# Two gated feed-forward layers: the second pair of result tiles in the second group computed by seven products, the preparation in fewer steps

## The chip, the cores and the metric

The kernel runs on one core of a Trainium2 chip. The metric is the device time of one execution in microseconds. The core's engines are TensorE (PE in the profile, its weight loads PEld), VectorE (DVE), ScalarE (ACT), GpSimd (POOL) and SyncE (SP), each with an instruction queue of its own that runs in order; they wait for each other through semaphores.

## The reference

Two blocks on 512 tokens of width 1024, in float32, the second with two layers:

```python
def first_block(x, ...):        # attention, HGRN2 recurrence and MLA branches, gated and merged, then
    x = x + jnp.square(jax.nn.relu(rmsnorm(x) @ w_ff1)) @ w_ff2
def second_block(x, ...):       # 2 layers: stick-breaking attention, differential attention
    x = x + mix
    x = x + (silu(h @ w_gate[i]) * (h @ w_up[i])) @ w_down[i]      # h = rms_norm(x, ffn_norm[i])
```

`w_gate` and `w_up` are 1024 x 2816, that is 22 result tiles of 128 columns each. The change concerns the two gated layers, the order of work in the preparation of all three feed-forward layers, and one detail of the recurrence.

## The kernel before

Everything is computed transposed: a tile is 128 features x 512 tokens. Each float32 operand is split into a high part (float32r) and a low part (the rest), and a product is high x high, low x high and high x low: three matmuls for one.

**Plain tiles.** A result tile ("rows" unit) takes 8 tiles of 128 inputs, 24 matmuls of 512 columns, issued in four pieces of six. Its weights come as a chunk of 512 KB (`raw`); ScalarE makes the high part (`split`, L1723, tile `wh`), VectorE the low part (`split_low`, `wl`). A gate tile is scaled by VectorE (L2262), goes through ScalarE's three steps of the sigmoid and is multiplied (`ev3`, L2328); an up tile is scaled and multiplied by the gate (L2318); then the result is split (tiles `R`). Output tiles ("out" units) are added to x by VectorE (L2430).

**Sevens.** A pair of neighbouring result tiles can be computed as a 2 x 2 block product with seven products instead of eight (class `Seven`): each product is 12 matmuls of 256 columns, 84 for the pair instead of 96 of that size. It needs four sums of the weights (S1 to S4, GpSimd, L2761, in the buffers `Q`, two of them in turn, filled by a 1 MB transfer each) and four sums of the tokens (T1 to T4, `sums`), each with a high and a low part. The products are, in this order: A12·B21, A11·B11, A22·T4, S1·T1, S2·T2, S4·B22, S3·T3. The weights' high parts (`wo_hi`) are ScalarE's, their low parts (`wo_lo`, tiles `wx` and `hl`) VectorE's, in four places in turn, made two to three products ahead. Partial results are combined by both (`wcp`, `wc`), and `wsig`, `wf`, `wf_hi`, `wf_lo` make the function's value. Product 6 of a seven is issued one piece later than the others, behind the next piece or behind product 0 of the next seven.

**The order.** A planner writes one list of steps; each engine's program takes its own steps from it in that order. `dense` walks through the pieces of a stage; behind each piece it lists the low parts pending (`low`), the steps deferred until now (`due`), the extra steps of this piece's number, and the eviction. `hgrn` gives the steps of the recurrence, which run between the pieces of the first gate/up group (`uGA`).

**The feed-forward layers** are stage 0 (first block), 1 and 2. `chain` orders them: all plain tiles of groups 0 and 1, the outputs of group 0, then sevens and outputs in turn. In stages 1 and 2 group 0 has two result tiles each of gate and up, group 1 four, all plain: 12 plain units of four pieces, 48 pieces; then 8 output pieces; then the first product. In stage 0 there are 8 plain units (32 pieces), and 16 output pieces. `preparation` places, by piece number: eight normed token tiles (`hn`, L2351, into `Q1`), the token sums (`t_sum`, L2362), their high (`t_hi`) and low parts (`t_lo`), the high and low parts of B21, B11 and B22 (`b_hi`, `b_lo`, into `hh` and `hl`, free after the last plain tile), and the first weights. The transfer for the second seven (`wq`) needs `Q1` and so waits for all of `b_lo`. In stages 1 and 2 the low part of T4 is placed at step 58, at the third product.

Of the kernel before, what the change touches and what calls it, by code (L numbers as in the profile page):

```python
# [192 lines left out]

PRODUCTS = (("A12", "B21"), ("A11", "B11"), ("A22", "T4"), ("S1", "T1"), ("S2", "T2"), ("S4", "B22"), ("S3", "T3"))
WEIGHT_PART = {n: i for i, n in enumerate(("A11", "A12", "A22", "A21", "S1", "S2", "S4", "S3"))}
TOKEN_SUMS = ("T1", "T2", "T3", "T4")
TOKEN_PARTS = {"B21": (4, 0), "B11": (0, 0), "B22": (4, 1)}
TOKEN_ORDER = ("B21", "B11", "B22")

# [111 lines left out]
class Plan:  # L311
# [89 lines left out]
            self.defer(9 + tt, "dt", u, tt)  # L401
        self.defer(5, "dn_root", u)

    def dense(self, units, more=None, crossed=False, hold=0):

        n, order, held = 0, [], []
        for u in units:  # L410
            if u.kind == "win":
                pieces = [(k, 0, 0) for k in range(7)]
            elif u.kind == "rows":
                pieces = [(0, j * u.nk + k, j * u.nk + k + 2) for j in range(u.n) for k in range(0, u.nk, 2)]
            else:
                pieces = [(i, a, a + 2) for i in range(4) for a in range(0, 8, 2)]
            order += [(u, piece) for piece in pieces]
        if crossed:
            order = order[:3] + order[4:6] + order[3:4] + order[6:]
        for i in range(len(order) - 1, 0, -1):  # L420
            if order[i - 1][0].kind == "win" and order[i - 1][1][0] == 6:
                order[i - 1], order[i] = order[i], order[i - 1]
        for i, (u, piece) in enumerate(order):
            tick, extra = self.low() + self.due(), (more or {}).get(n, [])
            after = order[i + 1][0] if i + 1 < len(order) else u
            n += 1
            if u.kind == "win":
                yield [("wp", u, piece[0])], self.seven(u, piece[0]) + tick + extra
                continue
            self.place(u)  # L430
            if u.kind == "rows" and piece[2] % u.nk == 0:
                steps = self.ready(u, piece[2] // u.nk - 1)
                if u.ev == "out" and after.kind == "win" and after.stage and steps[0][0] == "split":
                    self.defer(2, *steps.pop(0))
                    self.defer(4, *self.lows.pop())
                if n <= hold:
                    held.append(steps.pop())
                    tick += steps + extra
                else:
                    self.gated(u)  # L440
                    tick += steps[:-1] + extra + steps[-1:]
            else:
                tick += extra
            if held and n > hold:
                tick.append(held.pop(0))
                self.gated(tick[-1][1])
            if u.halved(piece[1] // u.nk) and piece[2] % u.nk:
                tick += [("ev_half", u), ("ship_half", u)]
            if u.kind == "cols" and piece[2] == 8:
                if piece[0] == 3:  # L450
                    tick.append(("ev", u))
                    if u.ev == "dq":
                        self.heads(u)
                tick += self.split(u.chunks[piece[0]] + 2)
            yield [("mm", u, *piece)], tick
        rest = self.due(True)
        if rest:
            yield [], rest
# [32 lines left out]
    def preparation(self, v, stage, wins, tick):  # L491

        more, w = {}, wins[0].v
        last_up = self.last_up[stage]

        def put(n, *step):
            more.setdefault(n, []).append(step)

        put(tick + 3, "wq", wins[0])
        plain = stage == 0  # L500
        end = 32 if plain else 48
        for m in range(8):
            put(((13, 14, 16, 17, 18, 20, 21, 22) if plain else (14, 15, 17, 18, 20, 21, 23, 24))[m], "hn", v, stage, m)
        put(14, "ws", wins[0])
        for k in range(4):
            put(((22, 24, 25, 27) if plain else (26, 28, 30, 32))[k], "t_sum", stage, k)
            put(((24, 25, 27, 28) if plain else (28, 29, 31, 33))[k], "t_hi", stage, k)
            put(((28, 30, 38, 40) if plain else (34, 36, 39, 58))[k], "t_lo", stage, k)
        put(29, "wo_hi", 7 * w)
        put(31, "wo_lo", 7 * w)  # L510
        put(30, "wo_hi", 7 * w + 1)
        put(end + 10 if plain else end - 1, "wo_lo", 7 * w + 1)
        for i in range(3):
            put(end + i, "b_hi", stage, i, last_up)
            put(end + 2 + i, "b_lo", stage, i)
        put(end + (9 if plain else 10), "wq", wins[1])
        put(end + (9 if plain else 10), "ws", wins[1])
        put(end + 3, "wo_hi", 7 * w + 2)
        return more
# [111 lines left out]
    def make(self):  # L631
# [23 lines left out]
        for idx, ff, e, norm in ((0, ff2a, 4, 4), (1, ff2b, 6, None)):  # L655
            for c in range(6):
                up, k0, nj, f = [], max(4 * c - 2, 0), 4 if c else 2, 8 + 6 * idx + c
                self.f_tile.append(tile)
                for j in range(nj if c < 2 else 0):
                    c0, wk = (k0 + j) * P, (k0 + j) % 8  # L660
                    gate = rows(("w_gate_2", idx), 0, 8, c0, P, ("h", e), "fgate", wk=wk)
                    up += [gate, rows(("w_up_2", idx), 0, 8, c0, P, ("h", e), "fup", gate=gate, wk=wk, f=f, j=j,
                                      tile=tile + j)]
                for j in ((), (), (0, 2))[min(c, 2)]:
                    c0 = (k0 + j) * P
                    gate = Seven(("w_gate_2", idx), c0, e - 1, 1 + idx, "gate")
                    up += [gate, Seven(("w_up_2", idx), c0, e - 1, 1 + idx, "up", gate=gate, f=f, j=j, tile=tile + j)]
                ff.append((up, self.out(("w_down_2", idx), k0, nj, ("f", f), norm=norm if c == 5 else None,
                                        ship=idx == 1 and c == 5)))
                tile += nj  # L670
# [89 lines left out]
        self.run(made[36:])  # L760
        self.banks = (0, 1)
        recurrence = list(self.hgrn())
        self.run(interleave(self.dense(uGA), iter(recurrence[:-4]), 44 / 48, False))
        self.banks = (0, 1, 4, 5)
        self.run(self.dense(uC, {2 + 2 * i: t for i, t in enumerate(recurrence[-4:])}))
        self.banks = (2, 3)
# [460 lines left out]
def tensor_program(pe, S, B, plan):  # L1227
# [84 lines left out]
    def seven(u, k):  # L1312

        i, (p, q) = u.product(k), u.banks()
        if k == 0:
            empty(q)
        elif k == 1:
            empty(p)
        elif k == 2:
            at.wait_ge("w_cp", 3 * u.v + 1)  # L1320
        elif k == 4:
            at.wait_ge("w_c", 3 * u.v + 1)
        elif k == 5:
            at.wait_ge("w_cp", 3 * u.v + 2)
        elif k == 6:
            at.wait_ge("w_cp", 3 * u.v + 3)
        first, second = slice(0, 256), slice(256, 512)
        out = {0: B.bank[q][:, first], 2: B.bank[q][:, first], 3: B.bank[q][:, second],
               5: B.bank[q][:, second]}.get(k, B.bank[p][:, first])
        (hi, lo), (high, low), name = B.operand(u.place(i)), B.tokens(PRODUCTS[k][1]), PRODUCTS[k][1]  # L1330
        ready = TOKEN_ORDER.index(name) + 1 + 3 * u.stage if name in TOKEN_ORDER else TOKEN_SUMS.index(name) + 1 + 4 * u.stage
        at.wait_ge("wo_hi", i + 1)
        at.wait_ge("b_hi" if name in TOKEN_ORDER else "t_hi", ready)
        for n in range(4):
            pe.matmul(out, hi[:, n, :], high[:, n, :], start=n == 0 and k not in (4, 5, 6), stop=False, skip_group_check=True)  # L1335
        at.wait_ge("b_lo" if name in TOKEN_ORDER else "t_lo", ready)
        for n in range(4):
            pe.matmul(out, hi[:, n, :], low[:, n, :], start=False, stop=False, skip_group_check=True)  # L1338
        at.wait_ge("wo_lo", i + 1)
        for n in range(4):  # L1340
            last = pe.matmul(out, lo[:, n, :], high[:, n, :], start=False, stop=n == 3, skip_group_check=True)  # L1341
        last.then_inc(S["w_mm"], 1)
        if k == 6:
            emptied[p], emptied[q] = (("w_c", 3 * u.v + 3),), (("w_c", 3 * u.v + 2),)
# [788 lines left out]
def vector_program(dve, S, B, plan):  # L2133
# [220 lines left out]
    def token_sums(stage, k):  # L2354
# [1 line left out]
        first, second = slice(0, 256), slice(256, 512)  # L2356
        at.wait_ge("hn", 8 * stage + (8 if k else 4))
        a, b = {0: (hn[:, 0:4, second], hn[:, 0:4, first]), 1: (hn[:, 4:8, second], B.token_sum(B.sums, 0)),
                2: (hn[:, 4:8, second], hn[:, 0:4, second]), 3: (hn[:, 4:8, first], B.token_sum(B.sums, 1))}[k]
        if k % 2:  # L2360
            at.wait_ge("t_s", 4 * stage + k)
        dve.tensor_tensor(out, a, b, ALU.subtract).then_inc(S["t_s"], 1)  # L2362

# [715 lines left out]
```

## Time and profile before

| | |
|---|---|
| median of 3 runs | 2114.66 us (2114.51 to 2117.36) |
| profiled execution | 2113.09 us, span 2111.3 us |
| TensorE busy | 2093.8 us, 99% of the span, 12528 matmuls |
| VectorE busy | 1471.9 us, 70% |
| ScalarE busy | 1054.5 us, 50% |
| GpSimd busy | 403.9 us, 19% |
| transfers of sevens | 44 of 1 MB |
| weight chunks | 244 of 512 KB |
| granted TensorE clock | full throughout |

Times in rows are microseconds from the start of the span. A matmul's duration in a row is longer than its pitch, since matmuls overlap; the pitch is read from the starts. In the rows the lines are those of helpers where a helper records the instruction: L2139 is every low part.

### The profile page before, as it was taken

What the parts mean: (1) busy time and instruction counts of PE and PEld (TensorE: products, weight loads), DVE (VectorE), ACT (ScalarE), POOL (GpSimd) and SP (SyncE); (2) the same over time, 40 slices, a digit from 0 to 9 for tenths busy, and PEclk for the clock granted to TensorE, in tenths of its full rate; (3) what the DMA queues carried; (4) which work ended last, traced back from release to release, by engine and by line L of the source; (5) the groups of instructions that cost most, each with busy time, mean ns of one, the idle gap of its engine ahead of it and who ended that gap; (6) DMA issues with size and microseconds to landing.
All of it is one profiled execution on the core that took longest, in us unless ns stands there. A gap on an engine that the chain in (4) does not pass through costs nothing.

```text
span 2111.3 us, 31641 instructions
## 1 busy us (share of the span) xinstructions
PE 2093.8 (99%) x12528; PEld 1732.0 (82%) x12528; DVE 1471.9 (70%) x2153; ACT 1054.5 (50%) x1798; POOL 403.9 (19%) x350
## 2 busy tenths in 40 slices
PE   9999999999999999999999999999999999999999
PEld 7768778778889898887777889999887667799998
DVE  5584774664587777664667888777656678878775
ACT  4463544554354343444555556555445565555553
POOL 0000432202012323010110134343011101134340
PEclk9999999999999999999999999999999999999999
DMA  4212112113242222222112332322221113232322
GB/s 173 81 60 90 51 55 95 50 64 126 90 140 93 107 99 102 67 94 80 51 60 70 110 111 90 120 90 90 80 90 60 60 41 110 90 120 91 114 107 70
DMA packets 45938, 187.18 MB, mean 89 GB/s; under 512 B 5216, under 2 KB 5728, under 8 KB 40032
## 3 DMA queue, kind: packets, MB, share of 16 engines
q1 hardware_dynamic: 45648, 184.98, 25.4%
q8 instruction: 100, 1.64, 0.3%
q14 instruction: 46, 0.38, 0.1%
q10 hardware_dynamic: 144, 0.18, 0.0%
HBM read 183.05 MB, written 2.10 MB: 88 GB/s over the span
## 4 chain that ended last, share of the span: by engine, by line
PE 91%; DVE 6%; ACT 2%; issue 1%; DMA 0%; SPq 0%; DVEq 0%; ACTq 0%
PE ps L1261 16%; PE ps L1264 15%; PE ps L1267 15%; PE ps L1338 7%; PE ps L1341 7%; PE ps L1335 7%; PE ps L1285 4%; PE ps L1288 4%; PE ps L1286 4%; PE ps L1240 3%; PE ps L1391 1%; PE ps L1443 1%; PE ps L1664 1%; PE ps L1646 1%; PE ps L1415 1%
## 5 line engine op out<-in xcount | busy, mean ns | idle before, releaser
L1723 ACT CAST wh<-raw 128x1024 fp32r<-128x1024 f32 (+1 forms) x246 | 257.6, 1047 | 324.3 <-PE ps L1267 237.6
L2761 POOL TENSOR_TENSOR Q<-Q 128x512 f32<-128x512 f32 x176 | 266.8, 1516 | 779.1 <-DMA Q<-in_sevens 768.8
L2139 DVE TENSOR_TENSOR wl<-raw,wh 128x1024 fp32r<-128x1024 f32 (+2 forms) x250 | 310.1, 1241 | 151.0 <-ACT wh L1723 150.6
L1261 PE MATMUL ps<-R,wh 128*128 128x512 f32 x892 | 286.5, 402 | 0.2 <-DVE W L2318 0.2
L1264 PE MATMUL ps<-R,wl 128*128 128x512 f32 x892 | 276.9, 391 | 0.5 <-DVE wl L2139 0.5
L1267 PE MATMUL ps<-R,wh 128*128 128x512 f32 x892 | 276.1, 390 | 0.0
L1261 PE MATMUL ps<-hh,wh 128*128 128x512 f32 x704 | 231.3, 409 | 1.3 <-DVE F L2277 0.7
L1264 PE MATMUL ps<-hh,wl 128*128 128x512 f32 x704 | 218.5, 392 | 0.9 <-DVE wl L2139 0.6
L1267 PE MATMUL ps<-hl,wh 128*128 128x512 f32 x704 | 217.6, 390 | 0.0
L1264 PEld LDWEIGHTS ps<-R,wl 128*128 128x128 f32 x892 | 167.1, 188 | 37.9 <-DVE wl L2139 1.9
L1267 PEld LDWEIGHTS ps<-R,wh 128*128 128x128 f32 x892 | 167.5, 188 | 36.2
L1261 PEld LDWEIGHTS ps<-R,wh 128*128 128x128 f32 x892 | 157.9, 189 | 35.2 <-issue 9.7
L2430 DVE TENSOR_TENSOR x<-ps,x 128x512 f32<-128x512 f32 x191 | 130.7, 688 | 76.4 <-PE ps L1267 74.0
L1264 PEld LDWEIGHTS ps<-hh,wl 128*128 128x128 f32 x704 | 131.7, 188 | 31.4 <-DVE wl L2139 3.2
L1261 PEld LDWEIGHTS ps<-hh,wh 128*128 128x128 f32 x704 | 125.4, 188 | 38.4 <-issue 15.1
L1267 PEld LDWEIGHTS ps<-hl,wh 128*128 128x128 f32 x704 | 132.1, 188 | 29.0 <-DVE hl L2220 0.3
L1285 PE MATMUL ps<-wh,hh 128*128 128x512 f32 (+1 forms) x384 | 155.1, 404 | 0.7 <-DVE F L2288 0.5
L2139 DVE TENSOR_TENSOR hl<-Q,hh 128x512 fp32r<-128x512 f32 (+1 forms) x163 | 147.4, 911 | 8.6 <-ACT hh L1849 8.6
L1288 PE MATMUL ps<-wh,hl 128*128 128x512 f32 (+1 forms) x384 | 148.8, 387 | 0.0
L1286 PE MATMUL ps<-wl,hh 128*128 128x512 f32 (+1 forms) x384 | 148.5, 387 | 0.0
L2139 DVE TENSOR_TENSOR wx<-Q,wx 128x512 fp32r<-128x512 f32 x154 | 133.9, 875 | 9.6 <-ACT wx L1849 9.6
L1897 ACT CAST R<-W 128x512 fp32r<-128x512 f32 x56 | 34.8, 622 | 152.8 <-DVE W L2395 83.5
(281 smaller groups left out, 3673.0 us busy)
## 6 DMA issues: line engine op xcount, KB each, us to landing
raw<-in_weights SPq DMA_DIRECT2D x244, 512.0 KB, 3.5
Q<-in_sevens SPq DMA_DIRECT2D x44, 1024.0 KB, 4.9
x<-in_x_t SPq DMA_DIRECT2D x4, 512.0 KB, 7.0
F<-in_x_t SPq DMA_DIRECT2D x4, 512.0 KB, 4.7
out<-x SPq DMA_DIRECT2D x7, 256.0 KB, 2.0
raw<-in_weights SPq DMA_DIRECT2D x4, 416.0 KB, 3.1
x<-in_bias SPq DMA_DIRECT2D x1, 1024.0 KB, 7.7
F<-in_weights SPq DMA_DIRECT2D x2, 384.0 KB, 3.5
```

What stands on the lines that cost most here:

```text
L1261: pe.matmul(out, hi[:, k, cs], B.tile(u.src, k)[0], start=k == 0, stop=False)
L1264: pe.matmul(out, lo[:, k, cs], B.tile(u.src, k)[0], start=False, stop=False)
L1267: last = pe.matmul(out, hi[:, k, cs], B.tile(u.src, k)[1], start=False, stop=k == u.nk - 1)
L1285: pe.matmul(out, B.hh[:, ts], hi[:, kk, :], start=k == 0, stop=False)
L1286: pe.matmul(out, B.hh[:, ts], lo[:, kk, :], start=False, stop=False)
L1288: last = pe.matmul(out, B.hl[:, ts], hi[:, kk, :], start=False, stop=k == 7)
L1335: pe.matmul(out, hi[:, n, :], high[:, n, :], start=n == 0 and k not in (4, 5, 6), stop=False, skip_group_check=True)
L1338: pe.matmul(out, hi[:, n, :], low[:, n, :], start=False, stop=False, skip_group_check=True)
L1341: last = pe.matmul(out, lo[:, n, :], high[:, n, :], start=False, stop=n == 3, skip_group_check=True)
L1723: act.copy(B.wh[s][:, 0:nk * ncol], B.raw[s][:, 0:nk * ncol]).then_inc(S["w_hi"], 1)
L2139: dve.tensor_tensor(lo, src, hi.bitcast(F32), ALU.subtract).then_inc(S[name], 1)
L2761: pool.tensor_tensor(B.weight_part(u.v, out), B.weight_part(u.v, a), B.weight_part(u.v, b), op).then_inc(S["w_s"], 1)
```

## The change

- In the two gated layers the second pair of group 1 (result tiles 2 and 3, gate and up) is computed by sevens: 36 sevens instead of 32 in these layers, 48 instead of 44 in all. In `chain` they come as gate, up and the first gate of group 2, one behind another, without an output unit between them.
- The preparation is placed for 32 plain pieces in all stages; `hn`, `t_sum`, `t_hi` stand a little earlier, and `wo_lo` of the second weight at step 39.
- The token sums are numbered T1, T2, T4, T3, and their low parts are made in the order in which the products use them: T4, T1, T2, T3.
- Beside the recurrence (`uGA`), the low part of a weight chunk is deferred by one piece (`behind`).

```diff
-TOKEN_SUMS = ("T1", "T2", "T3", "T4")
+TOKEN_SUMS = ("T1", "T2", "T4", "T3")
+SUMS_USED = (2, 0, 1, 3)
...
-            tick, extra = self.low() + self.due(), (more or {}).get(n, [])
+            tick, extra = self.due() if behind else self.low() + self.due(), (more or {}).get(n, [])
+            if behind:
+                for step in self.low():
+                    self.defer(1, *step)
...
-        end = 32 if plain else 48
+        end = 32
         for m in range(8):
-            put(((13, 14, 16, 17, 18, 20, 21, 22) if plain else (14, 15, 17, 18, 20, 21, 23, 24))[m], "hn", v, stage, m)
+            put((13, 14, 15, 16, 17, 18, 19, 20)[m], "hn", v, stage, m)
         put(14, "ws", wins[0])
         for k in range(4):
-            put(((22, 24, 25, 27) if plain else (26, 28, 30, 32))[k], "t_sum", stage, k)
-            put(((24, 25, 27, 28) if plain else (28, 29, 31, 33))[k], "t_hi", stage, k)
-            put(((28, 30, 38, 40) if plain else (34, 36, 39, 58))[k], "t_lo", stage, k)
+            put((21, 22, 24, 26)[k], "t_sum", stage, k)
+            put((22, 24, 26, 28)[k], "t_hi", stage, k)
+            put(((28, 38, 49, 51) if plain else (30, 38, 41, 43))[k], "t_lo", stage, SUMS_USED[k])
...
-        put(end + 10 if plain else end - 1, "wo_lo", 7 * w + 1)
+        put(end + 7, "wo_lo", 7 * w + 1)
...
-                for j in range(nj if c < 2 else 0):
+                for j in range(2 if c == 1 else nj if c == 0 else 0):
...
-                for j in ((), (), (0, 2))[min(c, 2)]:
+                for j in ((), (2,), (0, 2))[min(c, 2)]:
...
-        self.run(interleave(self.dense(uGA), iter(recurrence[:-4]), 44 / 48, False))
+        self.run(interleave(self.dense(uGA, behind=True), iter(recurrence[:-4]), 44 / 48, False))
```

The rest of the diff makes the waits of TensorE (`t_lo`) and the order of the token sums on VectorE follow the new numbering.

## Rows read from the trace of the kernel before

**Rows 1.** The page, part 1: busy time and share of the span by engine.

```profile
PE 2093.8 (99%) x12528; PEld 1732.0 (82%) x12528; DVE 1471.9 (70%) x2153; ACT 1054.5 (50%) x1798; POOL 403.9 (19%) x350
```

**Rows 2.** Waits of TensorE: total us, times, longest; the two longest of fifteen.

```profile
PE ps L1338 <- DVE sums_low L2139: 3.7, 2, 1.8
PE ps L1536 <- DVE F L2579: 3.7, 3, 1.5
```

**Rows 3.** TensorE in order of time, stage 1: start, us, line, tiles, count.

```profile
1154.46 0.62 PE L1261 MATMUL ps<-hh,wh 128*128 128x512 f32 x2
...
1165.35 1.02 PE L1359 MATMUL ps<-W,C 128*128 128x512 f32 x2
1165.81 1.03 PE L1261 MATMUL ps<-hh,wh 128*128 128x512 f32 x2
...
1232.02 0.64 PE L1335 MATMUL ps<-hh,wx 128*128 128x256 f32 x4
...
1238.43 0.64 PE L1335 MATMUL ps<-sums_high,hh 128*128 128x256 f32 x4
...
1239.87 0.64 PE L1335 MATMUL ps<-sums_high,wx 128*128 128x256 f32 x4
```

**Rows 4.** Busy time by window: PE, PEld, DVE, ACT, POOL, PEclk, DMA share, GB/s.

```profile
1177.94:1231.42 53.48, 53.41 (x236) 43.68 (x235) 47.66 (x59) 29.25 (x38) 1.82 (x2) 1.00 0.30 98
1779.52:1834.39 54.87, 54.11 (x235) 43.51 (x234) 48.69 (x58) 29.74 (x38) 4.48 (x3) 1.00 0.27 95
1278.00:1293.00 15.00, 15.00 (x108) 14.11 (x107) 11.92 (x15) 7.71 (x14) 6.39 (x4) 1.00 0.28 100
```

**Rows 5.** TensorE in order of time, stage 2.

```profile
1756.52 0.62 PE L1261 MATMUL ps<-hh,wh 128*128 128x512 f32 x2
...
1840.88 0.74 PE L1338 MATMUL ps<-sums_low,hh 128*128 128x256 f32 x4 [1.84 <-DVE sums_low L2139]
...
1841.93 0.64 PE L1335 MATMUL ps<-sums_high,hh 128*128 128x256 f32 x4
```

**Rows 6.** VectorE in order of time, stage 1, the preparation.

```profile
1207.60 0.69 DVE L2262 TENSOR_TENSOR ps<-ps,W 128x512 f32<-128x512 f32 x1
...
1224.48 1.28 DVE L2430 TENSOR_TENSOR x<-ps,x 128x512 f32<-128x512 f32 x2
...
1230.28 1.22 DVE L2139 TENSOR_TENSOR hl<-Q,hh 128x1024 fp32r<-128x1024 f32 x1
1231.42 2.48 DVE L2430 TENSOR_TENSOR x<-ps,x 128x512 f32<-128x512 f32 x4
```

**Rows 7.** GpSimd's weight sums, and VectorE's low parts away from and beside them, stage 1.

```profile
1219.94 0.68 DVE L2139 TENSOR_TENSOR wx<-Q,wx 128x512 fp32r<-128x512 f32 x1
...
1236.46 7.65 POOL L2761 TENSOR_TENSOR Q<-Q 128x512 f32<-128x512 f32 x4 [56.62 <-DMA Q<-in_sevens]
...
1237.24 1.78 DVE L2139 TENSOR_TENSOR wx<-Q,wx 128x512 fp32r<-128x512 f32 x1
...
1241.17 3.48 DVE L2139 TENSOR_TENSOR hl<-Q,hh 128x512 fp32r<-128x512 f32 x2
```

**Rows 8.** The page, part 5: the weight sums, mean ns of one.

```profile
L2761 POOL TENSOR_TENSOR Q<-Q 128x512 f32<-128x512 f32 x176 | 266.8, 1516 | 779.1 <-DMA Q<-in_sevens 768.8
```

**Rows 9.** The page, part 6: transfers of sevens, KB each, us to landing.

```profile
Q<-in_sevens SPq DMA_DIRECT2D x44, 1024.0 KB, 4.9
```

**Rows 10.** TensorE's first and last wait in the recurrence; VectorE ahead of the first.

```profile
262.10 0.62 PE L1267 MATMUL ps<-hl,wh 128*128 128x512 f32 x2
263.85 0.67 PE L1536 MATMUL ps<-F,W 64*64 64x32 f32 x32 [1.14 <-DVE F L2579]
...
306.31 0.67 PE L1536 MATMUL ps<-F,W 64*64 64x32 f32 x32 [1.51 <-DVE F L2579]
...
261.07 1.88 DVE L2139 TENSOR_TENSOR wl<-raw,wh 128x1024 fp32r<-128x1024 f32 x1
262.87 0.83 DVE L2579 TENSOR_TENSOR F<-F 128x256 f32<-128x256 f32 x1
```

More of the change, by code:

```diff
@@ L402, in heads, with dense @@
         self.defer(5, "dn_root", u)
-    def dense(self, units, more=None, crossed=False, hold=0):
+    def dense(self, units, more=None, crossed=False, hold=0, behind=False):
         n, order, held = 0, [], []
@@ L1330, in seven @@
         (hi, lo), (high, low), name = B.operand(u.place(i)), B.tokens(PRODUCTS[k][1]), PRODUCTS[k][1]
-        ready = TOKEN_ORDER.index(name) + 1 + 3 * u.stage if name in TOKEN_ORDER else TOKEN_SUMS.index(name) + 1 + 4 * u.stage
+        if name in TOKEN_ORDER:
+            made = ready = TOKEN_ORDER.index(name) + 1 + 3 * u.stage
+        else:
+            k_sum = TOKEN_SUMS.index(name)
+            made, ready = k_sum + 1 + 4 * u.stage, SUMS_USED.index(k_sum) + 1 + 4 * u.stage
         at.wait_ge("wo_hi", i + 1)
-        at.wait_ge("b_hi" if name in TOKEN_ORDER else "t_hi", ready)
+        at.wait_ge("b_hi" if name in TOKEN_ORDER else "t_hi", made)
         for n in range(4):
@@ L2358, in token_sums @@
         a, b = {0: (hn[:, 0:4, second], hn[:, 0:4, first]), 1: (hn[:, 4:8, second], B.token_sum(B.sums, 0)),
-                2: (hn[:, 4:8, second], hn[:, 0:4, second]), 3: (hn[:, 4:8, first], B.token_sum(B.sums, 1))}[k]
-        if k % 2:
+                2: (hn[:, 4:8, first], B.token_sum(B.sums, 1)), 3: (hn[:, 4:8, second], hn[:, 0:4, second])}[k]
+        if k in (1, 2):
             at.wait_ge("t_s", 4 * stage + k)
```

## The prediction

> **What bounds the kernel now.** I read the page first. TensorE is busy 99% of the span [rows 1], and its own waits are short [rows 2]: the two longest entries are 3.7 us each, one on the low parts of the token sums, one in the HGRN recurrence. So the time is TensorE's queue, and a change can gain only by giving it less to do or by taking out one of these waits; it loses whatever makes TensorE wait anew. The second view is the order in time of TensorE in the two gated layers. A piece of plain work (six matmuls of 512 columns) starts every 1.36 us (eight of them from 1154.46 to 1165.35); a product of a seven (twelve matmuls of 256 columns) every 1.44 us (1238.43 to 1239.87) [rows 3]. The third view, busy time by window, shows what the 99% hides: from the first normed tile of the preparation to the last low part of a token part, 53.5 and 54.9 us, VectorE is busy 47.7 and 48.7 us, 89% [rows 4]. VectorE is a queue in fixed order; the rest is mostly its waits for ScalarE's sigmoid. It is nearly full there, and this change shortens the stretch.
>
> **What TensorE loses there now.** In layer 1 of the second block (stage 1) the plain work starts at 1154.46, and the fourth product at 1238.43 [rows 3]. Without a wait it would be 56 pieces of 1.36, two statistics matmuls of 0.46 (1165.35 to the next piece, 1165.81) and three products of 1.44: 80.9 us, so 1235.4. Lost: 3.0 us, 0.9 of it ahead of the first product and 2.1 in the third, where the low part of T4 is late. In stage 2 the same count from 1756.52 gives 1837.5 against 1841.93 [rows 5]: lost 4.5. Together 7.5 us.
>
> **Part 1, fewer columns.** Per gated layer four plain tiles go (gate and up, two each): 16 pieces of 1.36 = 21.8 us. Two sevens come: 14 products of 1.44 = 20.2 us. Gain 1.6 us, in two layers 3.2 us. The first block's feed-forward layer keeps its split between plain tiles and sevens, whatever the change is called. ScalarE, DMA and the weight chunks (eight fewer of 512 KB, four more of 1 MB) have room: DMA is at 0.3 of its engines there [rows 4].
>
> **Part 2, the low parts in order of use.** T4's low part now stands at piece 30 instead of in the third product. That wait goes: 2.1 us in stage 1 as counted, and 2.0 in stage 2, where the row gives 1.84 for it [rows 5]; both are part of the 7.5. What is late next is part 3.
>
> **Part 3, the preparation in a shorter stretch.** The plain stretch shrinks from 48 to 32 pieces, so the first product moves 16 pieces nearer while all of the preparation stays. I follow VectorE's queue from the first normed tile, which keeps its time within the layer, to the low part of the second weight (step 39, just ahead of the first product). In the kernel before, the stretch up to the third low token part ends at 1231.42, 53.5 us after 1177.94 [rows 4]. Out of it go the two gate/up pairs between 1207.60 and 1224.48, 16.9 us [rows 6]. Three things inside these 16.9 us stay, and are put back: one of the two low token sums (1.14, the pitch of such an instruction from 1230.28 to 1231.42), the low part of the second weight (0.60), and, since the queue position is later, three more evictions of output tiles (0.60 each, from 2.48 for four that overlap a little). 53.5 - 16.9 + 1.1 + 0.6 + 1.8 = 40.1 us, so 1218.1. TensorE wants that low part in the last third of the second product: 0.46 + 40 x 1.36 + 1.44 + 0.96 = 57.3 us after 1154.46, 1211.7. Late by 6.4 us. Stage 2 from its own ends: 1834.39 - 1779.52 = 54.9, less the same 13.4, 41.5 us, so 1821.0, against 1756.52 + 57.3 = 1813.8 [rows 4, 5]: late by 7.3 us. Part of it will show earlier, as waits of single pieces for split weights (a chunk's low part behind two token sums, at piece 28) or for emptied banks (pieces 33 to 36); the sum up to the second product is what counts. Bounds: VectorE's own waits for the sigmoid inside the stretch (53.5 - 47.7 = 5.8 us) could partly be filled by the work now standing closer, which takes up to 3 us off each; nothing in the order removes the rest.
>
> **Part 4, three sevens in a row.** Behind the second product come sevens without output tiles between them. In its first six products VectorE has one eviction 0.6, six low parts 3.6, two low token sums 2.3, a chunk 1.1 and a combining step of 256 columns, taken at half of 0.6: 7.9 us in 8.6 us of TensorE. So it keeps its lateness, and GpSimd's four weight sums for the second seven meet it there: their weights land 4.9 us [rows 9] after the last low token part, which the count of part 3 puts at about 1214.5. ScalarE, busy 7.7 of 15 us in the steady part, keeps pace in 10.1. In the kernel before a low part of 0.6 us takes 1.7 beside such sums (the first row against the last two) [rows 7], 1.1 us more for each. Bounds per layer: 0 (it falls on slack, as in the steady part, where VectorE is busy 11.9 of 15 us and TensorE never waits [rows 4]), and 4 such delays less the 0.7 of slack, 3.7, with a share of a second group 5. I take 2.0, just over half of 3.7, since half of those instructions have one input in PSUM or fall beside a gap. The Trainium skill, SBUF — State Buffer, section "Who interferes with whom", says that a VectorE instruction with two SBUF inputs and a GpSimd instruction that reads SBUF block each other for a whole instruction. By that rule the trace's low parts agree, and the ceiling per group would be four whole sums; the total by it is 2126.4 us.
>
> **Part 5, the recurrence (split low parts a piece later).** Three times a 1.8 us low part of a weight chunk (261.07 to 262.87) stands ahead of the product that the recurrence's score waits for [rows 10]. TensorE loses 1.3 us at 263.85 (262.10 plus 0.46 was due), and alike at two later places, 306.31 the last: 3.7 us in all by the view of waits [rows 2], about 4.2 counted by starts as at the first. Moved behind it, the first is free; in the other two the next score hangs on the instruction right after the moved one, so some comes back. Bounds: gain 4.2, loss 1 where the low part now delays another score. I take a gain of 2.2, about half. The chunk is not wanted for more than four pieces, so its own lateness costs nothing.
>
> **Part 6, the first layer's preparation.** The same steps a little earlier or later, with the same 16 output pieces between. One token sum moves ahead of a chunk's low part: 0.3 us lost, within 0 and 0.6.
>
> **Sum.** New losses 6.4 + 7.3 + 2 x 2.0 = 17.7, instead of 7.5: +10.2. Columns -3.2, recurrence -2.2, first layer +0.3: +5.1 us. The profiled execution took 2113.09 us (span 2111.3), which gives 2118.2; it lies 1.6 us below the median of 2114.66, which the sum is moved to: 2119.8 us.
>
> **The rivals.**
> A. GpSimd's sums cost the row of sevens their full price: each of the four, 1.5 us [rows 8], holds one VectorE instruction for its whole length, 4 x 1.5 - 0.7 = 5.3 us per layer instead of 2.0. 2119.8 + 6.6 = 2126.4. For it: 1.78 us for one low part and 3.48 for two [rows 7]. Against: in the steady part TensorE bears such a group in every 15 us without a wait [rows 2, 4].
> B. VectorE's gaps take up much of the backlog: 3 us less in each layer, 2119.8 - 6.0 = 2113.8, no change to be measured. For it: the 5.8 us of gaps. Against: the sigmoid's waits are a chain inside each pair and stay.
> C, the other side. VectorE keeps pace: TensorE loses ahead of the sevens only what it loses now (0.9 and 2.5), the T4 waits of 4.1 go, and the columns and the recurrence give theirs: 2114.7 - 3.2 - 4.1 - 2.2 = 2105.2. It decides if VectorE's stretch, 40.1 us by my count, comes out under 34: the due time, 57.3 us, less the 23.5 at which it starts.
> D. The change does nothing for the first block's layer, as said; there is no chance to give it.
>
> **How the numbers follow.** Forecast 0.50 (own range 2115 to 2125), A 0.15, B 0.15, C 0.20. 0.2% is 4.2 us, about what a measurement of this kernel can tell from none. Slower (over 2118.9): seven tenths of the forecast and all of A, 0.50. Within: the rest of the forecast, 0.15, and most of B, 0.13: 0.28. Faster (under 2110.4): C and the edge of B, 0.22. The range 2106 to 2127 leaves out half of C and the upper half of A, and takes in both ends of parts 3 to 5.
>
> **What would show it.** In the changed profile: product pitch still 1.44; the list of waits led by TensorE on low parts of weights (wx, hl) in the second product and by chunks' low parts near piece 28, some 6 us per layer; no wait for T4; VectorE over 90% busy there; low parts of 1.7 us in the row of sevens; the recurrence's three waits down to one or two. Wrong would be: the second product on time in both layers.

## The result and the profile after

The changed kernel took 2131.52 us (median of 6 runs, 2131.15 to 2132.27) against 2114.59 us for the kernel before (6 runs, 2113.19 to 2117.36): ratio 1.008, 95% interval 1.0068 to 1.0092. It is 16.9 us slower. The direction was forecast, the size was not: 2119.8 us was predicted, and the range ended at 2127. The profiled execution took 2131.2 us (span 2129.5).

First the page of the kernel after, part 1, which answers to [rows 1]:

```profile
PE 2096.1 (98%) x12672; PEld 1737.8 (82%) x12672; DVE 1488.2 (70%) x2177; ACT 1065.9 (50%) x1830; POOL 436.0 (20%) x366
```

144 more matmuls (336 of 256 columns come, 192 of 512 go), and TensorE's share falls. The waits of TensorE after (total us, times, longest), against [rows 2]:

```profile
PE ps L1349 <- DVE hl L2147: 8.4, 3, 3.3
PE ps L1268 <- DVE wl L2147: 5.0, 6, 1.5
PE ps L1544 <- DVE F L2587: 2.6, 4, 1.0
PE ps L1349 <- DVE wx L2147: 2.3, 2, 1.7
PE ps L1265 <- DVE W L2326: 1.7, 2, 1.5
...
PE ps L1572 <- DVE F L2626: 0.9, 1, 0.9
```

The wait for T4's low part (`sums_low`) is gone. In its place stand low parts of weights, of sevens (`hl`, `wx`) and of chunks (`wl`). TensorE in order of time tells where, in stage 1 (lines are shifted by 4 to 8 against before):

```profile
1155.19 0.61 PE L1265 MATMUL ps<-hh,wh 128*128 128x512 f32 x2
...
1184.50 0.73 PE L1268 MATMUL ps<-hh,wl 128*128 128x512 f32 x2 [0.59 <-DVE wl L2147]
...
1196.87 0.73 PE L1268 MATMUL ps<-hh,wl 128*128 128x512 f32 x2 [1.09 <-DVE wl L2147]
...
1218.69 0.74 PE L1349 MATMUL ps<-hh,wx 128*128 128x256 f32 x4 [1.66 <-DVE wx L2147]
...
1230.06 0.75 PE L1349 MATMUL ps<-hh,hl 128*128 128x256 f32 x4 [3.34 <-DVE hl L2147]
...
1251.40 0.74 PE L1349 MATMUL ps<-hh,hl 128*128 128x256 f32 x4 [1.68 <-DVE hl L2147]
```

The layer starts 0.73 us later than before (1154.46). Then read two parts. Up to the second product, whose low part `wx` is late at 1218.69, is what the prediction called part 3. Behind it, in the row of sevens, come 3.34 and 1.68 us: part 4. I add up, over each stretch, what lies between the start of one group of matmuls and the next beyond 0.227 us for a matmul of 512 columns and 0.120 for one of 256. Each figure is good to about 0.1 us:

| us lost | stage 1, to the second product | behind it | stage 2, to the second product | behind it |
|---|---|---|---|---|
| before | 0.9 | 2.1 | 2.3 | 2.1 |
| after | 6.2 | 6.8 | 7.1 | 7.6 |

That is 27.7 instead of 7.4, so 20.3 us more; less 3.2 us for the fewer columns and plus 0.7 from before stage 1 this makes 17.8 us, and the spans differ by 18.2. In stage 2 the second product's own low part is hardly late (TensorE waits 0.15 us at 1830.33); the 7.1 us fall ahead of it, mostly in two waits for chunks' low parts (1.68 us before 1796.14, 1.27 before 1808.51), one for a bank that VectorE empties (1.63 before 1818.13) and one for which the view names no releaser (1.40 before 1815.04, right behind VectorE's L2336).

VectorE and GpSimd of the kernel after in the row of sevens, stage 1:

```profile
1217.95 0.68 DVE L2147 TENSOR_TENSOR wx<-Q,wx 128x512 fp32r<-128x512 f32 x1
...
1220.36 1.21 DVE L2147 TENSOR_TENSOR sums_low<-sums,sums_high 128x1024 fp32r<-128x1024 f32 x1
...
1221.83 3.14 DVE L2147 TENSOR_TENSOR wx<-Q,wx 128x512 fp32r<-128x512 f32 x2
1224.89 2.31 DVE L2147 TENSOR_TENSOR wl<-raw,wh 128x1024 fp32r<-128x1024 f32 x1
1227.12 2.28 DVE L2147 TENSOR_TENSOR sums_low<-sums,sums_high 128x1024 fp32r<-128x1024 f32 x1
1229.32 1.28 DVE L2147 TENSOR_TENSOR hl<-Q,hh 128x512 fp32r<-128x512 f32 x2
...
1220.04 8.28 POOL L2769 TENSOR_TENSOR Q<-Q 128x512 f32<-128x512 f32 x4 [39.35 <-DMA Q<-in_sevens]
```

The `hl` for which TensorE waits at 1230.06 is made at 1229.32. Ahead of it three rows take 7.5 us (1221.83 to 1229.32), which without GpSimd take 3.5. GpSimd's four sums run from 1220.04 to 1228.3. Busy time by window (columns as in [rows 4]), the preparation and the row of sevens:

```profile
1178.80:1218.60 39.80, 35.53 (x161) 28.19 (x159) 37.27 (x47) 21.48 (x29) 1.81 (x2) 1.00 0.30 98
1218.60:1257.00 38.40, 32.85 (x248) 31.10 (x249) 37.29 (x42) 20.84 (x39) 20.90 (x12) 1.00 0.25 88
```

VectorE is busy 94% of the one and 97% of the other. In the row, part of that busy time is standing still, since the same instructions are much shorter in e2 below. GpSimd's sums for the first seven reach into the preparation as well: three normed tiles take 3.11 us beside them in stage 1 (1178.80) and 4.14 in stage 2 (1789.41), where four of them take 2.73 away from them. The kernel before has such a group there too, and no run moves it, so what it costs in the preparation is not shown.

### The profile page after: what moved, and what is told of

The parts are those of the page before. It is cut to its first block, busy times and chain, and to the rows that moved or that the text cites. A ratio compares the mean times of both kernels' runs of the same rounds, so it can differ in the third digit from the quotient of the medians.

```text
span 2129.5 us, 32027 instructions
## 1 busy us (share of the span) xinstructions
PE 2096.1 (98%) x12672; PEld 1737.8 (82%) x12672; DVE 1488.2 (70%) x2177; ACT 1065.9 (50%) x1830; POOL 436.0 (20%) x366
## 4 chain that ended last, share of the span: by engine, by line
PE 87%; DVE 9%; ACT 2%; issue 1%; DMA 1%; SPq 0%; DVEq 0%; ACTq 0%
PE ps L1265 14%; PE ps L1268 14%; PE ps L1271 14%; PE ps L1349 7%; PE ps L1346 7%; PE ps L1343 7%; PE ps L1289 4%; PE ps L1292 4%; PE ps L1290 4%; PE ps L1244 3%; PE ps L1399 1%; DVE wl L2147 1%; PE ps L1451 1%; PE ps L1672 1%; DVE Q L2359 1%
## 5 line engine op out<-in xcount | busy, mean ns | idle before, releaser
L2769 POOL TENSOR_TENSOR Q<-Q 128x512 f32<-128x512 f32 x192 | 297.2, 1548 | 769.4 <-DMA Q<-in_sevens 758.0
L2147 DVE TENSOR_TENSOR wl<-raw,wh 128x1024 fp32r<-128x1024 f32 (+2 forms) x242 | 300.9, 1244 | 152.3 <-ACT wh L1731 151.7
L1265 PE MATMUL ps<-hh,wh 128*128 128x512 f32 x640 | 211.8, 412 | 1.7 <-DVE F L2285 0.7
L1268 PE MATMUL ps<-hh,wl 128*128 128x512 f32 x640 | 199.1, 392 | 4.8 <-DVE wl L2147 4.5
L1271 PE MATMUL ps<-hl,wh 128*128 128x512 f32 x640 | 197.8, 390 | 0.0
L2147 DVE TENSOR_TENSOR wx<-Q,wx 128x512 fp32r<-128x512 f32 x170 | 151.1, 895 | 9.6 <-ACT wx L1857 9.6
L1268 PEld LDWEIGHTS ps<-hh,wl 128*128 128x128 f32 x640 | 119.6, 188 | 33.4 <-DVE wl L2147 7.8
L1265 PEld LDWEIGHTS ps<-hh,wh 128*128 128x128 f32 x640 | 113.2, 188 | 36.7 <-issue 15.1
L1271 PEld LDWEIGHTS ps<-hl,wh 128*128 128x128 f32 x640 | 120.1, 188 | 26.5
L1857 ACT CAST hh<-Q 128x512 fp32r<-128x512 f32 x166 | 102.8, 621 | 42.2 <-PE ps L1349 42.2
```

The source lines that it names most:

```text
L1265: pe.matmul(out, hi[:, k, cs], B.tile(u.src, k)[0], start=k == 0, stop=False)
L1268: pe.matmul(out, lo[:, k, cs], B.tile(u.src, k)[0], start=False, stop=False)
L1271: last = pe.matmul(out, hi[:, k, cs], B.tile(u.src, k)[1], start=False, stop=k == u.nk - 1)
L2147: dve.tensor_tensor(lo, src, hi.bitcast(F32), ALU.subtract).then_inc(S[name], 1)
L2769: pool.tensor_tensor(B.weight_part(u.v, out), B.weight_part(u.v, a), B.weight_part(u.v, b), op).then_inc(S["w_s"], 1)
```

## The experiments

Two theories of the row of sevens stood at the start: contention (GpSimd's sums hold VectorE up) and a full queue (VectorE has more work of its own than the row has time). The experiments change the kernel after, except where the kernel before is named. Ratios are to the kernel before, with their 95% interval; what is taken from a trace is one execution of the run. The attempt to set the two new sevens apart (e4) gave no time, so whether their standing close together costs anything by itself is not shown.

**e1: the new order of the low parts alone, in the kernel before.**

```diff
-TOKEN_SUMS = ("T1", "T2", "T3", "T4")
+TOKEN_SUMS = ("T1", "T2", "T4", "T3")
+SUMS_USED = (2, 0, 1, 3)
...
-            put(((28, 30, 38, 40) if plain else (34, 36, 39, 58))[k], "t_lo", stage, k)
+            put(((28, 30, 38, 40) if plain else (34, 36, 39, 58))[k], "t_lo", stage, SUMS_USED[k])
```

> The kernel before with one part of the change alone: the low parts of the token sums in the order of use (T4, T1, T2, T3). Tiles, sevens, places of all other steps and the recurrence are those of before. My part 2: the T4 waits of 2.1 us and 2.0 us go and nothing else comes, 2114.6 - 4.1 = 2110.5 us. Rival: T1's low part, which now stands later, or the next low part in the queue is late instead and takes half or all of it back: 2112.5 to 2114.6 us. In the trace: the starts of the first product to the fourth in the second gated layer show which.

Measured: 2109.95 us, ratio 0.9975 (0.9965 to 0.9985). The two longest waits of TensorE left:

```profile
PE ps L1544 <- DVE F L2587: 3.7, 3, 1.5
PE ps L1252 <- POOL W L2737: 1.4, 1, 1.4
```

The T4 wait goes and nothing is late in its place: part 2 was right, and this part of the change by itself is the fastest version found, 4.8 us under the kernel before and 21.6 under the changed one.

**e2: GpSimd's sums of three sevens per layer made short (480 of their 512 columns are left out).**

```diff
+            n = 32 if u.stage and 0 < u.v - u.others[0].v < 4 else 512
-            pool.tensor_tensor(B.weight_part(u.v, out), B.weight_part(u.v, a), B.weight_part(u.v, b), op).then_inc(S["w_s"], 1)
+            pool.tensor_tensor(B.weight_part(u.v, out)[:, 0:n], B.weight_part(u.v, a)[:, 0:n], B.weight_part(u.v, b)[:, 0:n], op).then_inc(S["w_s"], 1)
```

> The changed kernel, in which GpSimd forms the weight sums of the second, third and fourth seven of the second and third gated layer on 32 of 512 columns only (the rest of these sums is left out). VectorE's work and order, transfers and TensorE's work stay. Contention theory (VectorE's instructions stand still while GpSimd adds in SBUF, and that is what the row of sevens lost, some 7 us per layer): most of that goes, 8 to 12 us less than the changed kernel, 2120 to 2123 us. Rival, the queue theory (VectorE simply has more work of its own than the row of sevens has time for): at most 3 us less, 2128.5 us or above. The lateness ahead of the second product, 5.7 and 6.5 us, stays by both.

Measured: 2118.46 us, ratio 1.0016 (1.0007 to 1.0025), 13.1 us less than the changed kernel and more than the contention theory had asked. The same instructions of VectorE as shown above, in this run, the window of the row, and GpSimd's first two groups:

```profile
1221.77 1.28 DVE L2147 TENSOR_TENSOR wx<-Q,wx 128x512 fp32r<-128x512 f32 x2
1222.97 1.22 DVE L2147 TENSOR_TENSOR wl<-raw,wh 128x1024 fp32r<-128x1024 f32 x1
1224.10 1.22 DVE L2147 TENSOR_TENSOR sums_low<-sums,sums_high 128x1024 fp32r<-128x1024 f32 x1
1225.24 1.28 DVE L2147 TENSOR_TENSOR hl<-Q,hh 128x512 fp32r<-128x512 f32 x2
...
1218.60:1257.00 38.40, 38.01 (x292) 36.73 (x293) 29.93 (x48) 25.75 (x46) 17.90 (x16) 1.00 0.29 104
...
1220.05 9.06 POOL L2770 TENSOR_TENSOR Q<-Q 128x32 f32<-128x32 f32 x4 [39.41 <-DMA Q<-in_sevens]
1231.42 2.02 POOL L2770 TENSOR_TENSOR Q<-Q 128x32 f32<-128x32 f32 x4 [2.31 <-DMA Q<-in_sevens]
```

VectorE starts at the same moment (1221.77 for 1221.83) with the same work, and the `hl` comes at 1225.24 instead of 1229.32. TensorE loses 0.8 us in the row of each layer instead of 6.8 and 7.6; up to the second product it loses what it did (6.1 and 7.3). VectorE, with six more instructions done, is busy 29.9 us instead of 37.3. So the row's loss is contention; VectorE's own work fits. That the sums are merely ready earlier is not the reason: the first short group ends at 1229.1, the full one ended at 1228.3. Beside VectorE's unbroken queue the four short sums take 9.06 us, the next group 2.02: here it is GpSimd that stands still. Of the 13.1 us, about 1.4 are not the delays themselves but the slow clock behind one of them (last section).

**e3: VectorE's low parts of the plain tiles' chunks made short (960 of 1024 columns are left out).**

```diff
+        m = 64 if plan.chunks[n][0] in ("w_gate_2", "w_up_2") else nk * ncol
-        low(B.wl[s][:, 0:nk * ncol], B.raw[s][:, 0:nk * ncol], B.wh[s][:, 0:nk * ncol], "w_lo")
+        low(B.wl[s][:, 0:m], B.raw[s][:, 0:m], B.wh[s][:, 0:m], "w_lo")
```

> The changed kernel, in which VectorE forms the low part of each weight chunk of the gated layers' plain tiles on 64 of 1024 columns only (the rest is left out): some 1.1 us less of VectorE work for each of ten chunks between a layer's start and its second product. Queue theory: VectorE's lateness ahead of the second product (5.7 and 6.5 us) goes, and since VectorE enters the row of sevens with time in hand, what the row lost goes too: 17 to 20 us less, 2112 to 2115 us. Contention theory: the lateness ahead of the second product goes, 12 us, but the row of sevens keeps its loss of some 7 us per layer beside GpSimd's sums: about 2119 us.

Measured: 2129.0 us, ratio 1.0065 (1.005 to 1.0081), 2.5 us less. Neither number came: the expectation counted ten such chunks, but behind 1199 the chunks are those of the output tiles, which this edit leaves whole. Four short ones fall between 1176 and 1196 and free about 4 us; VectorE spends 3 of them waiting for ScalarE, and the second weight's low part is only 1.3 us earlier:

```profile
1216.66 0.68 DVE L2147 TENSOR_TENSOR wx<-Q,wx 128x512 fp32r<-128x512 f32 x1
```

The row of sevens kept its wait of 3.3 us in each layer. That goes against the queue theory, though weakly, since VectorE enters the row only 1.3 us earlier. Of the 4 us taken out of the first half of the preparation a third arrives at the second product.

**e5: the recurrence's part alone, in the kernel before.**

```diff
-            tick, extra = self.low() + self.due(), (more or {}).get(n, [])
+            tick, extra = self.due() if behind else self.low() + self.due(), (more or {}).get(n, [])
+            if behind:
+                for step in self.low():
+                    self.defer(1, *step)
...
-        self.run(interleave(self.dense(uGA), iter(recurrence[:-4]), 44 / 48, False))
+        self.run(interleave(self.dense(uGA, behind=True), iter(recurrence[:-4]), 44 / 48, False))
```

> The kernel before with the recurrence's part of the change alone: in the weights that run beside the recurrence, the low part of a weight chunk is formed one piece later. All else is that of before. My part 5: 2.2 us less, 2112.4 us (bounds 2110.4 to 2115.6). Rival, which the profile of the changed kernel speaks for (its first plain piece of the first layer starts at 568.61 instead of 568.57): the three waits of the scores change shape and their sum doesn't, 2114.6 us.

Measured: 2114.72 us, ratio 1.0 (0.9991 to 1.0009). TensorE's waits:

```profile
PE ps L1539 <- DVE F L2582: 2.6, 4, 1.0
...
PE ps L1264 <- ACT wh L1732: 1.3, 1, 1.3
...
PE ps L1567 <- DVE F L2621: 0.9, 1, 0.9
```

The scores wait 2.6 us instead of 3.7, in four waits instead of three, and a new wait of 0.9 us appears in the recurrence at 266.70: 3.5 us instead of 3.7. (The entry of 1.3 us is not of the recurrence. It stands at 7.59 us, at the kernel's start, where the same matmul starts at 7.56 in the kernel before.) The rival was right: the waits change shape. The interval, about 1.9 us to either side, leaves out the gain of 2.2 only just; but the changed kernel too starts the first layer's plain work at 568.61 against 568.57 before.

**e6: GpSimd fills with zeros instead of adding (the same sums are left out).**

```diff
+            if u.stage and 0 < u.v - u.others[0].v < 4:
+                pool.memset(B.weight_part(u.v, out), 0.0).then_inc(S["w_s"], 1)
+            else:
...
```

> The changed kernel, in which GpSimd fills the weight sums of the second, third and fourth seven of the second and third gated layer with zeros over all 512 columns instead of adding (the sums are left out): it writes as much SBUF and reads none. The run with sums of 32 columns took 2118.5 us. If it is GpSimd's reading that holds VectorE up (the rule of the Trainium skill, SBUF - State Buffer, section 'Who interferes with whom'), this takes 2118 to 2120 us. Rival, any work of GpSimd on SBUF holds VectorE up, writing too: 2123 us or more.

Measured: 2118.28 us, ratio 1.0016 (1.0007 to 1.0025), as with 32 columns. GpSimd's group and VectorE beside it:

```profile
1220.37 2.28 POOL L2770 MEMSET Q<- 128x512 f32 x4 [39.28 <-DMA Q<-in_sevens]
...
1220.75 1.22 DVE L2147 TENSOR_TENSOR sums_low<-sums,sums_high 128x1024 fp32r<-128x1024 f32 x1
1221.88 0.42 DVE L2388 TENSOR_TENSOR W<-ps,W 128x256 f32<-128x256 f32 x1
1222.22 1.28 DVE L2147 TENSOR_TENSOR wx<-Q,wx 128x512 fp32r<-128x512 f32 x2
```

Neither is stretched: the four fills take 2.28 us in every group, and the low part inside them keeps its 1.2. A fill is also much shorter than a sum, so the run can't say how much of the 13 us is reading and how much is time; what it shows is that GpSimd's writing of the full width does no harm. The Trainium skill, SBUF — State Buffer, section "Who interferes with whom", says the same: a VectorE instruction with two SBUF inputs collides with a GpSimd instruction that reads SBUF, not with one that only writes.

**e7: the preparation earlier; e8: the same with short sums.**

```diff
-            put((13, 14, 15, 16, 17, 18, 19, 20)[m], "hn", v, stage, m)
+            put(((13, 14, 15, 16, 17, 18, 19, 20) if plain else (9, 10, 10, 11, 12, 13, 14, 15))[m], "hn", v, stage, m)
```

(the token sums from 16, their high parts from 17, T4's and T1's low parts at 24 and 26 in the same way; e8 has the short sums of e2 besides)

> The changed kernel with the preparation of the last two gated layers begun earlier: normed tiles from piece 9 instead of 13, token sums from piece 16 instead of 21, the first two low token parts at 24 and 26 instead of 30 and 38. No work is left out. Between 1168.6 and 1178.8 us VectorE stands idle for some 6 us there, waiting for ScalarE. Theory: these gaps take the normed tiles, and the lateness at the second product (5.7 and 6.5 us) falls by 4 to 5.5 us in each layer, while the row of sevens keeps its loss beside GpSimd's sums: 2121 to 2124 us. Rival, VectorE's stretch behind piece 28 is full whatever was done ahead of it (it waits there for the last plain piece before the token parts may be split): at most 3 us in all, 2128.5 us or more.

> The early preparation and GpSimd's sums on 32 of 512 columns (the rest of these sums left out) together. If the two losses are independent, both gains add up: the run with early preparation less 13.1 us. If the lateness ahead of the second product is all gone too, this is the price of the change without its two losses, the kernel with the new order of low parts (2110.0) less the columns (3.2) and plus the first layer's 0.7: 2107.5 us. Rival, one loss had hidden behind the other: 2112 us or more.

Measured: 2130.12 us, ratio 1.0072 (1.0058 to 1.0086), and 2117.11 us, ratio 1.0011 (1.0002 to 1.002): 1.4 us less than the changed kernel, and 1.4 less than e2. The sums' shortening brings 13.0 us here and 13.1 in e2, so the two losses are independent; but the first hardly moved, and e7 came within its rival's number. The second product is now late by 0.5 instead of 1.7 us; in exchange, TensorE and VectorE in e7 near 1180:

```profile
1181.24 0.73 PE L1268 MATMUL ps<-hh,wl 128*128 128x512 f32 x2 [2.71 <-DVE wl L2147]
...
1177.21 1.77 DVE L2359 SCALAR_TENSOR_TENSOR Q<-x,G,W 128x512 f32<-128x512 f32 x1
1178.90 0.69 DVE L2270 TENSOR_TENSOR ps<-ps,W 128x512 f32<-128x512 f32 x1
1179.50 1.68 DVE L2147 TENSOR_TENSOR wl<-raw,wh 128x1024 fp32r<-128x1024 f32 x1
```

A chunk's low part stands behind the normed tiles that were moved up, and a wait of 2.7 us comes there. Stage 1 loses 13.6 us in all, against 13.0.

**e9: the row's order; e10: VectorE's own sums; e11: both and a gentler early start.**

```diff
-                    self.defer(2, *steps.pop(0))
-                    self.defer(4, *self.lows.pop())
+                    row = after is after.others[0]
+                    self.defer(9 if row else 2, *steps.pop(0))
+                    self.defer(12 if row else 4, *self.lows.pop())
...
-            put(((28, 38, 49, 51) if plain else (30, 38, 41, 43))[k], "t_lo", stage, SUMS_USED[k])
+            put(((28, 38, 49, 51) if plain else (30, 38, 41, 45))[k], "t_lo", stage, SUMS_USED[k])
```

> The changed kernel with two of VectorE's instructions moved back inside the row of sevens of the last two gated layers: the weight chunk that is split there for plain work behind the row (its high part seven pieces later, its low part eight), and T3's low part from the third product to the last of the first seven. No work is left out, and GpSimd's sums stay. They stood ahead of the low part (1229.32) for which TensorE waits 3.5 us in each layer; both are stretched beside the sums, 2.31 and 2.28 us instead of 1.2. Theory: the row's loss is what VectorE's order lets GpSimd delay; the wait of 3.5 us goes in both layers and some of it comes back later in the row: 4 to 7 us less, 2124.5 to 2127.5 us. Rival, VectorE's total work beside the sums decides wherever it stands, and the loss moves down the row: 2130 us or more.

> The kernel of the run before (both instructions moved back), in which VectorE itself forms the weight sums of the second and third seven of each of the last two gated layers, four subtractions of some 0.6 us each, instead of GpSimd. No work is left out. Contention theory: such a group of GpSimd's delays VectorE by 3.9 us or more in the row; done by VectorE it costs 2.4 us, so 1.5 to 3 us less per group in time, up to 6 us less in all than that run while VectorE is behind. Rival: VectorE is so full there that its own 2.4 us are dearer than the delays, slower than that run.

> The kernel of the run before with the preparation begun a little earlier, in VectorE's gaps and less dense than in the early run: two normed tiles at pieces 9 and 10, the rest from 13, token sums from 19, T4's and T1's low parts at 28 and 33. No work is left out. If VectorE's gaps can be used, the lateness up to the second product (5.7 and 6.5 us) falls by 2 to 4 us in each layer; the sum over all would be 2112 to 2118 us. If every microsecond won is lost to a chunk's low part further ahead, as in the early run, within 1.5 us of the run before.

Measured: 2135.84 us (ratio 1.0102, 1.0087 to 1.0117), 2129.61 (1.0072, 1.0055 to 1.0089) and 2129.86 (1.0073, 1.0058 to 1.0088). e9 misses its theory and is slower than the changed kernel. e10 was expected up to 6 us under e9 and came 6.2 under. e11 came within 1.5 us of e10, the number for no gain. Rows of e10, TensorE and ScalarE:

```profile
1237.12 0.74 PE L1352 MATMUL ps<-hh,wx 128*128 128x256 f32 x4 [3.31 <-ACT W L1907]
...
1230.62 1.05 ACT L1740 CAST wh<-raw 128x1024 fp32r<-128x1024 f32 x1 [1.90 <-DMA raw<-in_weights]
```

The new wait is my edit's: the step `split` is SP's too. Nine pieces later it stands behind the loads of two sevens, which wait for their buffers, so ScalarE waits 1.9 us for the chunk, two sigmoids of three steps each follow, and the copy that frees TensorE's bank comes after them. e9 has this wait too, 2.87 us in stage 1 and 4.48 in stage 2. e10 against e9, with the same fault in both, is 6.2 us faster, but part of it is the clock, which stood at 0.50 for 3.3 us behind both of these waits in e9 and at full in e10; e12 and e13 below make the same comparison without that. e11's earlier start brought nothing.

**e12: only the two low parts moved; e13: with VectorE's own sums.**

```diff
-                    self.defer(4, *self.lows.pop())
+                    self.defer(12 if after is after.others[0] else 4, *self.lows.pop())
```

(T3's low part as in e9), and for e13:

```diff
+        for out, a, b, minus in SUM_STEPS:
...
+            dve.tensor_tensor(B.weight_part(u.v, out), B.weight_part(u.v, a), B.weight_part(u.v, b),
+                              ALU.subtract if minus else ALU.add).then_inc(S["w_own"], 1)
```

The step of the sums also stands four pieces later in e10, e11 and e13.

> The changed kernel with only VectorE's two low parts moved back inside the row of sevens: the chunk's low part by eight pieces, T3's from the third product to the last. The chunk's transfer and its high part stay where they are in the changed kernel; in the two runs before they had moved too, behind a load of seven weights on SP's queue, ScalarE waited 1.9 us for that chunk, and TensorE 3.0 and 4.6 us for ScalarE. Order theory: with that mistake mended, the wait of 3.5 us per layer becomes at most 1.8 us and nothing large follows, 2125 to 2128 us. Rival, the delayed work only moves down the row: 2130 us or more.

> The kernel of the run before, with the weight sums of the second and third seven of the last two gated layers formed by VectorE (2.7 us a group in the run with own sums) instead of GpSimd. No work is left out. Contention theory: a further 4 to 8 us less, 2119 to 2123 us, since the run with sums of 32 columns puts all of GpSimd's delays at 13.1 us and VectorE pays back 2.7 us for each of four groups only where it is behind. Rival, what VectorE takes over costs it as much as what it is spared: within 2 us of the run before.

Measured: 2128.36 us (ratio 1.0063, 1.0046 to 1.008) and 2123.25 (1.0039, 1.0024 to 1.0054). TensorE's waits in the row of stage 1 and just behind it, in e12:

```profile
1229.29 0.74 PE L1346 MATMUL ps<-sums_low,hh 128*128 128x256 f32 x4 [1.62 <-DVE sums_low L2147]
1236.62 0.74 PE L1343 MATMUL ps<-hh,wx 128*128 128x256 f32 x4 [0.36 <-ACT W L1897]
1241.18 0.74 PE L1349 MATMUL ps<-sums_high,hl 128*128 128x256 f32 x4 [0.46 <-DVE hl L2147]
...
1254.64 0.50 PE L1271 MATMUL ps<-R,wh 128*128 128x512 f32 x1 [1.54 <-DVE R L2147]
```

VectorE's order alone is worth 3.2 us of the changed kernel's time, just short of what the order theory had asked (2128 or less): 1.6 us of the 3.3 stay, a wait of 0.5 follows, and the 1.68 at 1251.40 comes back as 1.54 at 1254.64. Some of the 3.2 us is the clock: in the traces, the changed kernel loses 1.4 us to it in stage 2 (last section), e12 nothing. In e13 one group of sums takes VectorE 2.7 us:

```profile
1226.08 2.74 DVE L2394 TENSOR_TENSOR Q<-Q 128x512 f32<-128x512 f32 x4
```

and 5.1 us more are won; the row of stage 1 loses 3.3 us, against 6.8 in the changed kernel, 5.9 in e12 and 0.8 in e2. So half of the row's loss can be had back without leaving work out. The tiles by seven products still don't pay: up to the second product TensorE loses 6 to 7 us per layer as before the edits, for 1.6 us of columns.

## Why the prediction was right in direction and wrong in size

- **Part 1, columns**: right. The second seven's products keep the pitch of 1.44 us, and the sum of the losses with -3.2 us comes within 0.4 us of the spans' difference.
- **Part 2, T4**: right, shown alone by e1 (-4.8 us against -4.1 forecast).
- **Part 3, VectorE's queue late at the second product**: right in mechanism and size. The low part of the second weight ends 63.4 us after the layer's start (1217.95 + 0.60 - 1155.19); the working gave 63.6 (1218.1 - 1154.46). Up to there TensorE loses 6.2 and 7.1 us; 6.4 and 7.3 were forecast. In stage 2 it comes almost wholly ahead of the second product, as said above. Rival C, which needed a stretch under 34 us, falls: it measured 39.8 (1178.80 to 1218.60). So does rival B: the gaps of the preparation's first half are waits for ScalarE, and in e3 and e7 most of what is freed or moved there comes back as other waits.
- **Part 4, the row of sevens: the step that failed.** "I take 2.0", within 0 and 5 per layer; it measured 6.8 and 7.6, of which 0.8 each stays in e2 without the contention. The mechanism was named, its size was taken at less than a third. Three things were counted too low. The delays: I capped the first group at four low parts of 1.1 us less 0.7 of slack, but VectorE had no slack, being late already, and 4.0 us came through in full: 3.5 us at 1230.06, and 0.6 in two short waits at 1223.33 and 1225.02. The followers: I gave the second and third group a share inside the bound of 5, and they come while VectorE is still behind, for a further 1.7 us at 1251.40. And in stage 2 the clock, below. Rival A (5.3 us per layer, 2126.4 us) had the right mechanism and is still short by 1.5 and 2.3 us. I let the steady part, where TensorE bears a group every 15 us without a wait, outweigh it. The steady part has 3 us of VectorE time to spare in 15. Without the contention the row as a whole would have nearly that share, 4.75 of 28.80 us (e2, from 1219.20), but none in its first 8.8 us, and that is where the first group falls.
- **Part 5, the recurrence**: wrong, 0 instead of -2.2. e5 shows it alone: part came back as other waits in the recurrence, 3.5 us in all for 3.7. Its bounds held.
- **Part 6, the first layer**: 0.7 instead of 0.3, outside its bounds of 0 and 0.6 by little. The token sum ahead of a chunk's low part costs 0.4 us before 608.83, as foreseen; a place that the working left out costs 0.5 before 597.54, where three normed tiles instead of two now stand ahead of a chunk's low part.

The profiled time was forecast as 2118.2 and came as 2131.2, 13.0 us more: part 4 has 10.4 of it (14.4 instead of 4.0), part 5 2.2, part 6 0.4, part 3 -0.4; 0.4 is not accounted for.

## What to carry to other kernels

Price a contention by the state of the engine that it hits. In the steady part of this kernel, where VectorE has slack, a group of sums costs nothing; in the row, where it is already late, the first group's delay arrived in full, and more came with the next. (The groups also stand closer there, and no run separates the two.) Test an edit in its parts: here a reordering of four instructions gains 0.25% alone, and was buried under tiles that cost 22 us. In a planner like this one, a step that is moved takes its parts on every engine with it; move the one instruction, not the step.

## What the runs showed of the hardware that I had not expected

A pause of TensorE can cost more than itself. In stage 2 of the kernel after it waits 3.34 us (until 1841.70), and the window behind it reads:

```profile
1841.70:1845.00 3.30, 3.30 (x19) 3.30 (x20) 3.03 (x6) 1.24 (x3) 0.00 (x0) 0.67 0.48 137
```

The granted clock is 0.67 on average in these 3.3 us, between its two levels of 1.2 and 2.4 GHz, and groups of four matmuls start every 0.85 us instead of 0.48 up to 1846.1: 1.4 us lost on top. The equally long pause of stage 1 was followed by full clock. In the traces of all the runs, nine of the fourteen waits of 2.7 us or more were followed by such a stretch, and so were two of the shorter ones (1.77 us in e7 at 1791.46: 0.72 over 3.3 us; 1.61 us in e9 at 1229.30: 0.57). So the same wait of 3.34 us costs 3.3 us in one place and 4.7 in another, and no row here says beforehand which.

Nor does the slow stretch always cost time. In e7 the wait of 2.71 us at 1181.24 is followed by a clock of 0.60, in e8 the same wait by full clock, and both lose 6.0 us up to the second product of stage 1, where VectorE and not TensorE sets the pace.
